# State-space layer: tokens stationary in feed and readout, its output turned by TensorE instead of by way of DRAM, its blocks in the array's quadrants with the skip term in them

## The reference, cut to what matters

```python
def s5_mixer(h, a_re, a_im, log_dt, b_re, b_im, c_re, c_im, d_skip, w_glu):
    ...
    def per_sequence(u_s):
        bu_re = jnp.einsum('sgc,gpc->sgp', u_s, bb_re)
        bu_im = jnp.einsum('sgc,gpc->sgp', u_s, bb_im)
        _, _, x_re, x_im = lax.associative_scan(
            _scan_combine, (a_seq_re, a_seq_im, bu_re, bu_im), axis=0)
        return jnp.einsum('sgp,gcp->sgc', x_re, cr) - jnp.einsum('sgp,gcp->sgc', x_im, ci)

    y = lax.map(per_sequence, u).reshape(B, S, D)
    y = y + d_skip.astype(F32) * h.astype(F32)
    g = jax.nn.gelu(y).astype(h.dtype)
    val, gate = jnp.split(g @ w_glu, 2, axis=-1)
    return val * jax.nn.sigmoid(gate)
```

## Time and profile before

| | |
|---|---|
| median of 3 runs | 2895.3 us (2889.72 to 2903.58) |
| profiled execution, its own time | 2897.61 us |
| its span | 2895.8 us |
| mean granted clock of TensorE | 0.997 of full speed |
| TensorE busy | 2864.4 us (99%) |
| VectorE, ScalarE, GpSimd busy | 1880.5, 1418.6, 392.1 us |
| the 16 rounds in the span | from about 1884 to 2001 us |

### The profile page before, as it was taken

The page is one execution under the profiler, slowest core; times in us unless marked ns, Lnnn a source line. Parts: engine busy times, 40 slices in busy tenths (PEclk is TensorE's granted clock), DMA queues, the critical chain, the costliest instruction groups (busy, mean ns, idle before and its releaser), DMA issues.

```text
span 2895.8 us, 45438 instructions
## 1 busy us (share of the span) xinstructions
PE 2864.4 (99%) x19070; PEld 2613.0 (90%) x19070; DVE 1880.5 (65%) x2575; ACT 1418.6 (49%) x1964; POOL 392.1 (14%) x445
## 2 busy tenths in 40 slices
PE   8999999999999999999999999999999999999998
PEld 8999988998899988989998899898889999988997
DVE  6998655766566656778665666588555555555555
ACT  5444645556555555444444445654445444444444
POOL 0000000000000000008872754043000000000000
PEclk9999999999999999999999999999999999999999
DMA  7565455552555545557776676585655555655553
GB/s 243 191 195 168 159 189 187 188 179 91 175 189 175 175 162 178 190 198 244 239 246 215 228 235 206 189 251 159 216 182 189 198 189 192 200 190 191 196 195 131
DMA packets 288043, 558.45 MB, mean 193 GB/s; under 512 B 27424, under 2 KB 35872, under 8 KB 287584
## 3 DMA queue, kind: packets, MB, share of 16 engines
q1 hardware_dynamic: 281376, 531.27, 56.0%
q0 software_dynamic: 5600, 22.78, 2.0%
q10 hardware_dynamic: 864, 1.50, 0.2%
HBM read 530.34 MB, written 25.17 MB: 192 GB/s over the span
## 4 chain that ended last, share of the span: by engine, by line
PE 92%; DVE 4%; ACT 2%; issue 1%; DMA 0%; POOL 0%; SPq 0%; ACTq 0%; DVEq 0%; POOLq 0%
PE G L506 87%; PE T L506 4%; DVE WL L1660 1%; ACT WH L1074 1%; DVE Y L1668 1%; PE T L585 1%; PE G L983 0%; ACT SC_e L1077 0%; DMA WB<-s_w 0%; DVE ST L1741 0%; DVE SC_e L1668 0%; DMA X<-in_x 0%; ACT L1071 0%; POOL ZZ L2438 0%; PE T L913 0%
## 5 line engine op out<-in xcount | busy, mean ns | idle before, releaser
L1660 DVE TENSOR_TENSOR WL<-RAW,WH 128x1024 fp32r<-128x1024 f32 (+1 forms) x948 | 1185.0, 1259 | 751.4 <-ACT WH L1074 741.8
L1074 ACT ACTIVATE WH<-RAW 128x1024 fp32r<-128x1024 f32 (+1 forms) x948 | 994.3, 1056 | 1024.1 <-PE G L506 1023.7
L506 PE MATMUL G<-A1h,WH 128*128 128x256 f32 (+1 forms) x2587 | 720.7, 280 | 3.2 <-DVE WL L1660 2.2
L506 PE MATMUL G<-A1l,WH 128*128 128x256 f32 x2560 | 713.1, 279 | 0.0
L506 PE MATMUL G<-A1h,WL 128*128 128x256 f32 x2560 | 711.7, 278 | 0.0
L506 PEld LDWEIGHTS G<-A1h,WH 128*128 128x128 f32 x2587 | 486.9, 189 | 7.1 <-DVE WL L1660 3.4
L506 PEld LDWEIGHTS G<-A1l,WH 128*128 128x128 f32 x2560 | 484.0, 189 | 0.4
L506 PEld LDWEIGHTS G<-A1h,WL 128*128 128x128 f32 x2560 | 483.3, 189 | 0.0
L506 PE MATMUL G<-WH,Bh 128*128 128x512 f32 x1024 | 399.3, 390 | 0.3 <-DVE WL L1660 0.3
L506 PE MATMUL G<-WH,Bl 128*128 128x512 f32 x1024 | 398.5, 389 | 0.0
L506 PE MATMUL G<-WL,Bh 128*128 128x512 f32 x1024 | 398.5, 389 | 0.0
(11 more groups left out here) (326 smaller groups left out, 3565.0 us busy)
## 6 DMA issues: line engine op xcount, KB each, us to landing
RAW<-in_mlp_w SPq DMA_DIRECT2D x256, 1024.0 KB, 5.5
RAW<-in_even_w_in SPq DMA_DIRECT2D x52, 1024.0 KB, 5.2
RAW<-in_a_w_in SPq DMA_DIRECT2D x48, 1024.0 KB, 5.2
RAW<-in_b_w_glu SPq DMA_DIRECT2D x32, 1024.0 KB, 5.4
RAW<-in_odd_w_in SPq DMA_DIRECT2D x20, 1024.0 KB, 5.1
RAW<-in_even_w_out SPq DMA_DIRECT2D x16, 1024.0 KB, 5.1
RAW<-in_odd_w_out SPq DMA_DIRECT2D x16, 1024.0 KB, 5.0
RAW<-in_a_w_out SPq DMA_DIRECT2D x16, 1024.0 KB, 5.0
```

The costliest lines, as they stand in the source:

```text
L506: return e.matmul(out, lhsT, rhs, start=start, stop=stop, skip_group_check=True)
L1074: return e.activation(out, in_, ACT.Copy, scale=scale, bias=0.0)
L1660: return e.tensor_tensor(out, a, b, op)
```

## The change

- `within`: the four block products of a round go to the four quadrants of 32 rows of a bank, the loop over re/im outside the one over m. Four small matmuls of an identity slice with a 32-column diagonal `DD` add the skip term to the diagonal blocks. `DD` and `EYE` are built once on GpSimd, after the last `SPR` store.
- ScalarE copies the bank once, whole (`KD`, 128 x 128). SP writes it to DRAM (`KR`, 64 KB, `blocks_out`), waits, and places it in `FD` by four DMAs (`blocks_placed`).
- `feed` and `readout`: `US` and `ZX` (the former `ZZ` for this use, 64 columns) are stationary, `FD` and `RD` (128 columns) streamed, and the results go to the upper or lower 64 rows of the bank. They come one round later for `feed`: `feed(a - 1)` just before `readout(a - 1)`.
- The output is turned by eight matmuls of 64 x 64 with an identity (`turn_y`) after the gelu, from `YG` to the free half of the bank. The trip through DRAM (`gelu_out`, `gelu_back`), VectorE's `output`, GpSimd's `DU` and the 16 small copies for `DST` are gone.
- The decay factors `MG` are made by ScalarE (`decay`, four copies of 64 columns each) and not by GpSimd.
- The last two rounds' tiles are finished between the first blocks of `gl0`.

```diff
@@ -991,9 +991,13 @@
                 e.wait_ge(*(n_h["s", 4 + a] if a < 4 else f_c[a - 2]))
+            if a == 0:
+                e.wait_ge(*eye["d"])
+            for i in range(2):
+                for m in range(4):
+                    mm(T[32 * m:32 * m + 32, 0:128], W[:, i, m, 96:128], R[:, i, m, 0:128], i == 0, False)
             for m in range(4):
-                for i in range(2):
-                    tk = mm(T[0:32, 128 * m:128 * m + 128], W[:, i, m, 96:128], R[:, i, m, 0:128], i == 0, i == 1)
+                tk = mm(T[32 * m:32 * m + 32, 0:32], IDENT[:, 32 * m:32 * m + 32], DD[:, a, :], False, True)
             tk.then_inc(*f_mm.up(a))
...
         def feed(a):
-            e.wait_ge(*f_c[a])
+            e.wait_ge(*k_back[a % 2][a])
             if a >= 2:
-                e.wait_ge(*y_sum[a - 2])
-            for m in range(4):
-                tk = mm(G[a % 2][:, 64 * m:64 * m + 64], FD[a % 2][:, m, :], US[:, 4 * a + m, :], m == 0, False)
+                e.wait_ge(*g_low[a - 2])
+            for h in range(2):
+                for g in range(2):
+                    m = 2 * g + h
+                    tk = mm(G[a % 2][64 * g:64 * g + 64, 128 * h:128 * h + 128], US[:, 4 * a + m, :], FD[a % 2][:, m, :],
+                            h == 0, False)
             tk.then_inc(*fd_mm.up(a))
 
         def readout(a):
             e.wait_ge(*x_sum[a])
-            for m in range(4):
+            for h in range(2):
                 for i in range(2):
-                    tk = mm(G[a % 2][:, 64 * m + 1:64 * m + 64], RD[a % 4][:, i, m, 32:160], ZZ[a % 2][:, i, 64 * m:64 * m + 63],
-                            False, i == 1)
+                    for g in range(2):
+                        m = 2 * g + h
+                        tk = mm(G[a % 2][64 * g:64 * g + 64, 128 * h:128 * h + 128], ZX[a % 2][:, i, m, :],
+                                RD[a % 4][:, i, m, 32:160], False, i == 1)
             tk.then_inc(*y_mm.up(a))
+
+        def turn_y(a):
+            e.wait_ge(*gelu[a])
+            T, Yg = G[a % 2], YG[a % 2]
+            for j in range(4):
+                for g in range(2):
+                    ps = slice(64 * g, 64 * g + 64)
+                    tk = mm(T[ps, 256 + 64 * j:320 + 64 * j], Yg[ps, 64 * j:64 * j + 64], IDENT[ps, ps], True, True)
+            tk.then_inc(*y_t.up(a))
...
                 turn_w(a + 1)
-            feed(a)
-            if 1 <= a < 15:
                 within(a + 1)
+            if a >= 2:
+                turn_y(a - 2)
             if a:
+                feed(a - 1)
                 readout(a - 1)
...
+            copy(KD[a % 2], block_bank(a)[:, 0:128]).then_inc(*f_c.up(a))
+
+        def decay(a):
+            if a >= 2:
+                e.wait_ge(*scan[a - 2])
+            for m in range(4):
+                d = copy(MG[a % 2][:, 64 * m:64 * m + 64], KEEP[:, :], M4[:, 4 * a + m:4 * a + m + 1])
+            d.then_inc(*mg.up(a))
...
+        def blocks_out(a):
+            e.wait_ge(*f_c[a])
+            e.dma_start(KR[a], KD[a % 2]).then_inc(*k_out[a % 2].up(a, 16))
+
+        def blocks_placed(a):
+            e.wait_ge(*k_out[a % 2][a])
+            if a >= 2:
+                e.wait_ge(*fd_mm[a - 2])
+            else:
+                e.wait_ge(*zeros["fd"])
+            v = KR[a].rearrange("(m c) x -> c m x", c=32)
             for j in range(4):
-                e.dma_start(v[j], by_pair(YG[a % 2][32 * j:32 * j + 32, :])).then_inc(*y_out[a % 2].up(a, 16))
...
+                e.dma_start(FD[a % 2][32 * j:32 * j + 32, :, 32 * j:128], v[:, :, 0:128 - 32 * j]).then_inc(
+                    *k_back[a % 2].up(a, 16))
...
-            for a in range(20):
+            for a in range(16):
+                if a >= 2:
+                    blocks_placed(a)
                 if a < 14:
                     drive_matrices(a + 2)
                 if a == 0:
+                    blocks_out(0)
+                    blocks_out(1)
+                    blocks_placed(0)
+                    blocks_placed(1)
+                if a == 1:
                     stacks(3)
                 if 2 <= a < 14:
                     readout_matrices(a + 2)
-                if a >= 4:
-                    gelu_back(a - 4)
-                if 3 <= a < 19:
-                    gelu_out(a - 3)
+                if 1 <= a < 15:
+                    blocks_out(a + 1)
                 if a in (3, 5, 7, 9):
                     load(gl0 + (a - 3) // 2)
```

More of the change, by code:

```diff
@@ L206, in build_program @@
     M4 = sb("M4", [128, 64], ctx=ctxs)
-    DST = sb("DST", [128, 64], ctx=ctxs)
+    sb("pad_dst", [128, 64], ctx=ctxs)
     RBS = sb("RBS", [128, 64], ctx=ctxs)
@@ L222, in build_program @@
     CTD = [VAR5[:, 2048 + 256 * i:2304 + 256 * i].rearrange("p (a b) -> p a b", b=16) for i in range(2)]
-    YS, DU, MG, YG = ([VAR5[:, 512 * n + 256 * i:512 * n + 256 * i + 256] for i in range(2)] for n in range(4))
-    YB = [VAR5[:, 2048 + 256 * i:2304 + 256 * i] for i in range(4)]
+    MG, YG = ([VAR5[:, 512 * n + 256 * i:512 * n + 256 * i + 256] for i in range(2)] for n in (2, 3))
+    DD = VAR5[:, 0:512].rearrange("p (a b) -> p a b", b=32)
+    KD = [VAR5[:, 512 + 128 * i:640 + 128 * i] for i in range(2)]
+    EYE = VAR5[:, 768:800]
+    ZX = [VAR5[:, 2048 + 512 * i:2560 + 512 * i].rearrange("p (i a b) -> p i a b", i=2, b=64) for i in range(2)]
     MAG = M4[:, :]
@@ L410, in build_program @@
     stack = [sig(f"stack{i}") for i in range(4)]
-    y_out = [sig(f"y_out{i}") for i in range(2)]
-    y_back = [sig(f"y_back{i}") for i in range(4)]
+    y_t = sig("y_t")
     u_sc = sig("u_sc")
-    du = sig("du")
+    eye = sig("eye")
+    k_out = [sig(f"k_out{i}") for i in range(2)]
+    k_back = [sig(f"k_back{i}") for i in range(2)]
     mg = sig("mg")
@@ L1039, in pe, with last_tiles @@
                 turn_w(a + 1)
-            feed(a)
-            if 1 <= a < 15:
                 within(a + 1)
+            if a >= 2:
+                turn_y(a - 2)
             if a:
+                feed(a - 1)
                 readout(a - 1)
+        def last_tiles():
+            turn_y(14)
+            yield
+            feed(15)
+            readout(15)
+            yield
+            yield
+            turn_y(15)
+            yield
+        beside(last_tiles())
         on_pair[0], on_pair[1] = "s5_y", "s5_w"
         for i in range(4):
-            gemm(f"gl{i}", A1h, A1l, None if i else (lambda kt: e.wait_ge(*g_low[kt])),
-                 None if i else (lambda: readout(15)), 1)
+            gemm(f"gl{i}", A1h, A1l, None if i else (lambda kt: e.wait_ge(*g_low[kt])))
             gemm(f"gg{i}", A1h, A1l)
@@ L1577, in act @@
         mlp(0, "s", HT, lambda k: col("norm_mix", 16 + k), first_matrices)
+        e.wait_ge(*zeros["keep"])
+        e.wait_ge(*d_step["m4"])
+        decay(0)
         turned(1)
@@ L2510, in pool @@
             e.dma_start(SPR[a], STR).then_inc(*sp_r.up(a, 16))
+        for m in range(4):
+            if m:
+                e.wait_ge(*eye[m - 1])
+                tt(EYE, EYE, IDENT[:, 32 * m:32 * m + 32], ALU.add).then_inc(*eye.up(m))
+            else:
+                e.tensor_copy(EYE, IDENT[:, 0:32]).then_inc(*eye.up(m))
+        e.wait_ge(*eye[3])
+        tt(DD, EYE.unsqueeze(1).to_broadcast([128, 16, 32]), col("b_d", 0, 16).unsqueeze(2).to_broadcast([128, 16, 32]),
+           ALU.mult).then_inc(*eye.up("d"))
         e.wait_ge(*c_io["c"])
@@ L2534, in inputs @@
             tt(US[:, m, :], US[:, m, :], RBS[:, :].unsqueeze(1).to_broadcast([128, 4, 64]), ALU.mult).then_inc(*u_sc.up(a))
-            e.wait_ge(*u_sc[a])
-            if a >= 2:
-                e.wait_ge(*y_sum[a - 2])
-            tt(by_pair(DU[a % 2]), US[:, m, :], DST[:, m].unsqueeze(2).to_broadcast([128, 4, 64]), ALU.mult).then_inc(*du.up(a))
-            if a >= 2:
-                e.wait_ge(*scan[a - 2])
-            tt(MG[a % 2].rearrange("p (a b) -> p a b", b=64), KEEP[:, :].unsqueeze(1).to_broadcast([128, 4, 64]),
-               M4[:, m].unsqueeze(2).to_broadcast([128, 4, 64]), ALU.mult).then_inc(*mg.up(a))
+        for i in range(2):
+            e.memset(ZX[i][:, :, :, 0:1], 0.0)
         e.wait_ge(*d_step["rbs"])
```

91 lines of the change are left out of this document (28 added, 63 removed).

## The result

The changed kernel takes 2902.15 us (median of 20 runs, 2895.0 to 2906.4), the kernel before 2894.29 us (median of 20 runs, 2888.99 to 2903.58). The ratio is 1.0025 with a 95% interval of [1.0017, 1.0033]: slower by about 7 us. That is less than the 0.5% that the prediction called measurable, though 20 runs of each do tell it from nothing. The forecast was 2909; the range (2892 to 2930) holds the time, but the move is only half of the +14 that was forecast.

What follows compares the result with a forecast made beforehand. TensorE bound the kernel before; SP's wait for its store would set the rounds after. Start +1, middle +9.9, end -5.4 and +1.7, clock +7: +14 us on the profiled 2897.6, median about 2909, range 2892 to 2930.

Steps and rivals of the forecast that it cites:

- The added wait: SP's queue, each round: store lands 5.4 to 6.9 us after RD's issue, making rounds 8.3 us; +9.9 us over 11 rounds.
- TensorE's and VectorE's part: Work per round: TensorE falls from 7.30 to 5.4 to 5.8 us, VectorE to 5.7 to 6.6 us.
- The clock: TensorE's clock falls to 1.2 GHz inside the rounds, for about a third of them; +7 us.
- The start: Up to the end of round 3: blocks' store and placement precede WB loads in SP's queue; +1 us.
- The end: After readout(13): -5.4 us up to gl0's first matmul, then +1.7 us for work moved into gl0's blocks.
- A: The forecast case: SP's wait sets 7.7 to 9.2 us a round, clock falls part-time; +3 to +25 us, chance 0.50.
- B: Rival: same SP wait, but the clock stays up; 7.7 to 8.3 us a round, 0 to +7 us, chance 0.22.

Runs made afterwards that it cites:

- The pair of kernels with 640 KB more: Changed kernel plus an unread 640 KB DRAM copy in SP's queue, just ahead of the blocks' store (2918.89 us) or just behind it (2904.55 us).
- The kernel with the clock kept up: Changed kernel with 14 more transposes of the identity, leaving no result, behind the drive of rounds 1 to 14; 2901.71 us.

## Why the prediction was half right

- **The added wait: right.** SP waits for the landing of its store 12 times in 91 us, its largest wait; a round takes 91.1/11 = 8.28 us, and 8.3 was forecast. The landing takes 4.7 us in the median from the store's own issue, so it is 5.1 from RD's, a little under the low end of my 5.4 to 6.9; the mean round comes out the same in part because five of SP's issues take 1.4 to 1.6 us instead of 0.4, and three times in the 11 rounds the chain goes through WB, transposes, products and copy instead. The pair of kernels with 640 KB more shows that it is the place in the queue that costs.
- **TensorE's and VectorE's part: right.** 5.65 us of work where 5.4 to 5.8 was forecast: feed 0.49, readout 0.97, turn 0.61, block products with skip 0.64 us. Halves and quadrants do run side by side. VectorE is busy for 58.63/11 = 5.3 us a round, below the 5.7 to 6.6 of the forecast.
- **The clock: this step failed.** "If the clock is down for about a third of the rounds, that is 11 x 1/3 x 2.0 = +7." The clock was down for about a quarter of the time, but it cost nothing that can be measured. The 2.0 us in that product is what a round of 10.3 us has over SP's 8.3; it holds only for a round that is slow from end to end, and none is. The falls here are short: the work of a round grows from 5.65 to at most 8.0 us (in the round from 1941.11 to 1952.15), which is still under SP's 8.28, so the 2.6 us of waiting take it up. TensorE's waits show it: 17.8/11 = 1.6 us a round are left of the 2.6. The prediction had set the slow work against SP's round, as it should, but had taken a third of the time at half speed for a third of the rounds at half speed. The kernel with the clock kept up has the same time to 0.4 us. In two places slow work does stand in the chain (the transposes from 1935.90, 1.97 us and not 1.04; turn, feed and readout from 2004.79, 3.32 us and not 2.1). By these rows I estimate 2 us for both, under what the runs can tell apart.
- **The start: right in kind, too small.** +3.3 and not +1. The clock was at half from 1884.6 to 1898.2 us (a drive took 3.4 us from start to start instead of 1.8), which the prediction did not have; but the delay there is again SP's: the store of the blocks for round 2 was issued at 1902.52, right behind the last inputs' copies, its placement done at 1908.1, WB for round 4 issued at 1908.20 (forecast 1906), and TensorE stood for 5.26 us until 1911.50. In the kernel with more transposes the first two drives ran at full clock, and the stretch from the first drive to the fifth took 31.1 us, against 30.4 in the changed kernel and 25.9 before. So counted from the first drive the start is 4.5 us longer, of which 1.0 is hidden in the table, since the first drive began that much sooner.
- **The end: right to 0.1 us up to gl0, wrong behind it.** -5.4 as forecast. Behind the first matmul of gl0 I had +1.7 and it was -1.2. In the earlier trace rows the clock of before is at half until 2009.4, 5 us into gl0, at 2.5 us of lost work; after the change the clock is full again from 2007.5, before gl0 begins. I had read those rows for the cost of a fall and not for what the fall already cost the kernel before.
- Without the clock's term the forecast's sum was +7, and the measured difference is 7. That is luck in part: +2.3 at the start and -2.9 at the end cancel. Of the prediction's cases, A describes the mechanism (the wait, and a clock that falls) and B the time.

Where did the expected gain go? TensorE's work in a round fell by 1.65 us (7.30 to 5.65), VectorE's by about 1.7 (7.0 to 5.3). Two of the three parts kept it: with tokens stationary and the output turned by TensorE, but the blocks made and copied as before, the kernel is 11 us faster than before. The third part, the quadrants with the blocks' trip through DRAM, costs 19 us net of what it saves TensorE, since it puts a wait for this round's result in front of the next round's loads.

## What to carry to other kernels

A round trip through DRAM is cheap only if no in-order queue that feeds the loop waits for it: count the whole circle (issue, landing behind what was sent before, next issues, landing of the loads, compute, copy), and know that moving the wait to another place in the queue or to another engine's queue makes a new circle. Price a slow clock only where the slowed engine sets the pace; where it waits anyway, the waits pay for it, as long as the slow work of a round still fits into the round. When a small product must be spread over partitions, take the widest packing whose copies the free engine can still carry: two groups with eight copies beat four groups with sixteen copies by 18 us, and one group with four by 11.

## What was unexpected of the hardware

**A queue of its own does not put a small store ahead of the loads.** In ScalarE's queue, with nothing ahead of it there, the 64 KB store landed after 3.7 us in the median and 4.9 to 5.2 us when WB, RD and a 1 MB load had been sent by SP shortly before or just behind it; in SP's queue it was 4.7 us behind them and 2.6 us ahead of them. The Trainium skill, "DMA: Bandwidth & Descriptors", section Queues, rings and completion order, has two rules on this: each DMA engine takes turns between the queues, and the increment that reports a DMA's end lands only after every earlier write of that DMA engine, across its queues. The first alone would let the store by; the second fits what the rows show, though no run here separates the two.

**VectorE's adds took 0.77 us beside GpSimd and take 0.42 alone.** Before the change, VectorE's two adds stood at the same time as GpSimd's, and the scans beside GpSimd's multiplication. VectorE's and GpSimd's timelines of the kernel before (start us, us, instruction):

```profile
1945.97 1.55 DVE L1660 TENSOR_TENSOR XX<-XX,ZZ 128x256 f32<-128x256 f32 x2
1947.55 1.68 DVE L2327 TENSOR_TENSOR_SCAN ZZ<-VAR,XX 128x256 f32<-128x256 f32 x2
```

```profile
1945.65 1.59 POOL L2438 TENSOR_TENSOR ZZ<-XX 128x256 f32<-128x256 f32 x2
1947.20 0.90 POOL L2438 TENSOR_TENSOR US<-US,RBS 128x256 f32<-128x256 f32 x1
```

and in the kernel with the decay back on GpSimd, where GpSimd's work of the round stands beside other instructions of VectorE (GpSimd from 1940.48 to 1943.15):

```profile
1942.14 0.65 DVE L1692 TENSOR_TENSOR A1l<-G,A1h 128x256 fp32r<-128x256 f32 x1 [1.73 <-ACT A1h L1102]
1942.68 0.69 DVE L1692 TENSOR_TENSOR XX<-T,TC 128x512 f32<-128x512 f32 x1
...
1944.00 0.76 DVE L1692 TENSOR_TENSOR XX<-XX,ZZ 128x256 f32<-128x256 f32 x2
```

The two adds are 1.55 us together in the first and 0.76 us in the second. The instructions that stand beside GpSimd here read one operand from PSUM, and take what they always take. The Trainium skill, "SBUF — State Buffer", section SBUF: two separate sides, gives a rule that fits in part: VectorE and GpSimd exclude each other for an instruction of VectorE with two operands in SBUF while GpSimd reads SBUF. The rows show less than whole instructions taken in turns: alone, VectorE's two adds (0.76 us) and GpSimd's two (1.40 us in the kernel with the decay back) would need 2.16 us, and before the change all four were done in 1.87 us (1945.65 to 1947.52). This is read from overlaps; no kernel here moved GpSimd's adds alone.
